# Four weight buffers one word further each, the activations right behind them, and two masks read as one spread column

## The chip, the cores and the metric

The kernel runs on one core of a Trainium2 chip. The time is the device time of one execution in microseconds (us); smaller is better. A core has a matrix engine (TensorE, PE in the rows; its weight loads are PEld), a vector engine (VectorE, DVE), a scalar engine (ScalarE, ACT), a small general engine (GpSimd, POOL) and a queue engine (SyncE, SP). All of them work on one on-chip memory of 128 partitions, in which every tensor has a byte address that is the same in each partition.

## The reference

The reference is a float32 forward pass over 256 tokens of width 1024: two model blocks after each other. The first has an attention layer with compressed, selected and windowed keys (NSA), a convolutional feed-forward layer, a state-space layer (SSD) and a second feed-forward layer. The second has a gated delta rule layer (GDN) with attention to a memory, and a gated feed-forward layer. Cut to what matters here:

```python
def conv_ffn(h, w_up, conv_w, conv_b, w_down):
    u = causal_dwconv(h @ w_up, conv_w, conv_b)
    val, gate = u[..., :FFN_HIDDEN], u[..., FFN_HIDDEN:]     # FFN_HIDDEN = 2816
    return (jax.nn.silu(gate) * val) @ w_down

x = x + rms_norm(mixer(rms_norm(x, g0)), g1)                 # NSA, then SSD, then GDN + memory
x = x + rms_norm(ffn(rms_norm(x, g2)), g3)                   # three times
```

Nearly all arithmetic is in the products of the 256 rows with some 45 million weights, each of which is read once.

## The kernel before

The weights come as 176 chunks of up to 2048 columns by 128 partitions, in the order in which they are used. SyncE loads chunk i into `raw[i % 3]`. ScalarE rounds it into `whi[i % 4]` (L520) and VectorE, for 12 chunks GpSimd, writes the rest, raw minus high, into `wlo[i % 4]` (L528, L536). The activations are held in the same two parts, transposed, in `xT[0]` and `xT[1]` for the input of a layer, in `gT` for the hidden layer of a feed-forward part, in `yT` and `yG` for the outputs of SSD and GDN, and in `mT` for the memory rows. Every product is then three matmuls (L539 to L541, `pe_three`), which add up in the same bank of the accumulators:

```python
def pe_three(e, out, a, b, start, stop):
    e.matmul(out, a[1], b[0], start=start, stop=False)
    e.matmul(out, a[0], b[1], start=False, stop=False)
    return e.matmul(out, a[0], b[0], start=False, stop=stop)
```

The first operand is loaded into the array as weights (stationary, 128 columns), the second is streamed past it (moving). In the rows `bank<-xT,whi` means that `xT` is moving and `whi` is stationary. There are three uses:

- `pe_fm`: a piece of the chunk is stationary (128 columns) and `xT[:, k, :]` is moving (256 columns). The two loops over 22 chunks in each feed-forward part ("up") are of this kind, as are most projections.
- `pe_tm`: `xT[:, k, 128 s:128 s + 128]` is stationary and a chunk piece of 256 columns is moving.
- `pe_down`: a piece of `gT`, `yT`, `yG` or `xT` is stationary and 512 columns of a chunk are moving.

Each matmul has a weight load of its own, and the load of the next runs while the present one streams. The steps in `k` are 1024 bytes apart in the operands with 256 columns, the two halves of a piece 512 bytes. The order of the layers' pieces is written out by hand for each engine in NSA, SSD and GDN; the feed-forward parts are plain loops.

Where the tensors lie follows from the order in which they are declared, each rounded up to 32 bytes. In bytes from the start of a partition, with the remainder of a division by 512 that the prediction uses:

| tensor | before | remainder | after | remainder |
|---|---|---|---|---|
| `whi[i]` | 41088 + 8192 i | 128 | 41088 + 8196 i | 128 + 4 i |
| `wlo[i]` | 73856 + 8192 i | 128 | 74368 + 8196 i | 128 + 4 i |
| `xT[0]`, `xT[1]` | 128960, 137152 | 448 | 108096, 116288 | 64 |
| `masks` | 110144 | 64 | 152576 | 0 |
| `gT` | 157760, 180288 | 64 | the same | 64 |
| `yT`, `yG`, `mT` (all six) | 157760 to 211008 | 64 | the same | 64 |

`half` holds two masks of 128 by 128, ones in the rows of the lower or of the upper 64 partitions. They are stationary operands of L1685, L1686 and L2228 alone.

Of the kernel before, what the change touches and what calls it, by code (L numbers as in the profile page):

```python
# [97 lines left out]
    _ROWS[_n] = (_o, _w)  # L98
    _o += _w
_NROW = _o  # L100
_MASKS = 6 * 128 + 8 * 64 + 8


def _host_masks():

    a = np.arange(128)
    r, c = a[:, None], a[None, :]
    same = (r // 64) == (c // 64)
    m = [r == c, r <= c, (r <= c) & same, same, (r < 64) & (c >= 0), (r >= 64) & (c >= 0)]
    m = [x.astype(np.float32) for x in m]  # L110

    r, c = r % 64, np.arange(64)[None, :]
    for b in (1, 2, 4, 8, 16, 32):
        m.append(((r // (2 * b) == c // (2 * b)) & (r % (2 * b) < b) & (c % (2 * b) >= b)).astype(np.float32))
    m += [(r == c).astype(np.float32), (r <= c).astype(np.float32)]

    m.append((a[:, None] // 15 == np.arange(8)[None, :]).astype(np.float32))
    return np.ascontiguousarray(np.concatenate(m, 1))
# [138 lines left out]
PW, NRAW, NHL, AHEAD = 1024, 3, 4, 3  # L257


def build(nc, wall, x_d, mem_d, cols_d, rows_d, masks_d, neg_d, out_d):  # L260
    f32 = mybir.dt.float32
    f32r = mybir.dt.float32r
# [17 lines left out]
    with root:  # L280
# [20 lines left out]
        def sb(shape, dt=f32, st=root, name="t"):  # L301
            names[0] += 1
            return st.enter_context(nc.sbuf_tensor(f"{name}{names[0]}", shape, dt))
# [2 lines left out]

        banks = [root.enter_context(nc.psum_tensor(f"bank{i}", [128, 512], f32)) for i in range(8)]
        raw = [sb([128, 2048], name="raw") for _ in range(NRAW)]
        whi = [sb([128, 2048], f32r, name="whi") for _ in range(NHL)]
        wlo = [sb([128, 2048], f32r, name="wlo") for _ in range(NHL)]  # L310
        cols = sb([128, _NCOL], name="cols")
        masks = sb([128, _MASKS], name="masks")
        negf_w = 2 * 128 + 64 + 30 + 8 + 4 + 1
        negb = sb([128, negf_w - 1], bf16, name="negb")
        identb = sb([128, 128], bf16, name="identb")
        valid = sb([128, 2], name="valid")
        srow = sb([128, 32 + 32 + 16], name="srow")
        grow = sb([128, 1024], name="grow")
        nhalf = sb([128, 1], name="nhalf")
        h = sb([128, 2, 1024], name="h")  # L320
        xT = [sb([128, 8, 256], f32r, name="xT") for _ in range(2)]
        ss = sb([128, 8], name="ss")
        rr = sb([128, 4], name="rr")
        sqj = sb([128, 1024], name="sqj")
        xs = sb([128, 1024], name="xs")
        grow2 = sb([128, 1024], name="grow2")
        sb([128, 16], name="space")
        gains = (grow, grow2)
        ident, tri, tri64, blk64 = (masks[:, 128 * i:128 * i + 128] for i in range(4))
        half = [masks[:, 512:640], masks[:, 640:768]]  # L330
        level, (idc, tric) = ([masks[:, 768 + 64 * i:832 + 64 * i] for i in v] for v in (range(6), range(6, 8)))
        ones1 = masks[:, 255:256]
        own8 = masks[0:120, 1280:1288]
        neg_qk, neg_sl, neg_gd = negb[:, 0:128], negb[:, 128:256], negb[:, 256:320]
        quad, fourth = negb[0:96, 350:358], negb[0:96, 358:362]

# [112 lines left out]
        for i in range(2):  # L449
            c = {n: sb([128, 4, 128], st=gd, name=n) for n in ("kbg", "kg", "vb")}  # L450
# [2677 lines left out]
```

## Time and profile before

| | |
|---|---|
| three runs | 1198.19, 1198.83, 1201.48 us; median 1198.83 |
| the profiled execution, its own time | 1202.38 us |
| its span, from the first to the last instruction | 1200.6 us |
| TensorE busy | 1174.5 us, 98% of the span |
| VectorE, ScalarE busy | 847.7 us, 652.0 us |
| granted TensorE clock, mean | 0.999 |
| instructions | 23183 |

A busy TensorE is not TensorE at its peak: matmuls overlap, and each is shown with its whole latency (some 280 ns for 256 columns), so its pace is read from the start of one to the start of the next, or by counting how many fall into a stretch.

### The profile page before, as it was taken

To read this page: it belongs to the slowest core of one execution; us is meant where nothing else is said; L and a number is where in the kernel's file an instruction comes from. 1 tells how busy PE (TensorE), PEld (TensorE's weight loads), DVE (VectorE), ACT (ScalarE), POOL (GpSimd) and SP (SyncE) were. 2 spreads that over 40 slices of the span, in tenths; PEclk is the share of its full clock that TensorE was granted. 3 is DMA by queue.
4 is the path that set the end of the run, shared out by engine and by line. 5 is a ranking of instruction groups with operands and counts; after the bars stand their busy time and mean duration, and the time that the engine had idled before them with its cause. 6 is when DMAs were issued, how large, how long until landed. Compare 5 with 4: busy or idle time off the path is not lost.

```text
span 1200.6 us, 23183 instructions
## 1 busy us (share of the span) xinstructions
PE 1174.5 (98%) x9852; PEld 1078.0 (90%) x9852; DVE 847.7 (71%) x1299; ACT 652.0 (54%) x1171; POOL 151.1 (13%) x143
## 2 busy tenths in 40 slices
PE   8999999999999999999999999999999999999998
PEld 8897789999889898878999988999989878999986
DVE  6678777888557988886788865857577776655542
ACT  4657556666446665744666643665434534645431
POOL 1320000000002332100000000103443401000000
PEclk9999999999999999999999999999999999999999
DMA  8832235565634453352755564452231322755540
GB/s 308 269 141 89 100 104 206 189 210 195 231 106 176 155 183 137 115 184 106 281 180 195 188 233 170 170 185 106 104 110 72 111 94 97 281 186 197 181 174 35
DMA packets 31622, 196.67 MB, mean 164 GB/s; under 512 B 4000, under 2 KB 5664, under 8 KB 9376
## 3 DMA queue, kind: packets, MB, share of 16 engines
q1 hardware_dynamic: 27504, 185.17, 43.6%
q10 hardware_dynamic: 4016, 10.03, 2.6%
q8 instruction: 77, 1.26, 0.4%
q14 instruction: 25, 0.20, 0.0%
HBM read 193.09 MB, written 1.05 MB: 162 GB/s over the span
## 4 chain that ended last, share of the span: by engine, by line
PE 88%; DVE 5%; ACT 3%; issue 2%; POOL 1%; DMA 0%; DVEq 0%; POOLq 0%; ACTq 0%
PE bank L539 24%; PE bank L540 24%; PE bank L541 24%; DVE wlo L528 2%; PE bank L1895 1%; PE bank L1133 1%; PE bank L1190 1%; PE bank L1217 1%; ACT whi L520 1%; PE bank L726 1%; PE bank L2539 1%; PE bank L2482 1%; PE bank L3006 1%; POOL rr L668 0%; PE bank L2497 0%
## 5 line engine op out<-in xcount | busy, mean ns | idle before, releaser
L528 DVE TENSOR_TENSOR wlo<-raw,whi 128x1024 fp32r<-128x1024 f32 x322 | 389.1, 1245 | 88.8 <-ACT whi L520 88.1
L539 PE MATMUL bank<-xT,wlo 128*128 128x256 f32 x1488 | 419.0, 282 | 4.3 <-DVE wlo L528 2.1
L541 PE MATMUL bank<-xT,whi 128*128 128x256 f32 x1488 | 413.7, 278 | 0.0
L540 PE MATMUL bank<-xT,whi 128*128 128x256 f32 x1488 | 413.4, 278 | 0.0
L520 ACT ACTIVATE whi<-raw 128x1024 fp32r<-128x1024 f32 (+1 forms) x349 | 349.3, 1048 | 116.4 <-PE bank L541 89.9
L539 PEld LDWEIGHTS bank<-xT,wlo 128*128 128x128 f32 x1488 | 279.1, 188 | 7.9 <-DVE xc L1602 2.8
L540 PEld LDWEIGHTS bank<-xT,whi 128*128 128x128 f32 x1488 | 279.4, 188 | 0.6 <-issue 0.5
L541 PEld LDWEIGHTS bank<-xT,whi 128*128 128x128 f32 x1488 | 279.3, 188 | 0.0
L668 POOL TENSOR_TENSOR rr<-rr,nhalf 128x1 f32<-128x1 f32 x34 | 24.8, 730 | 710.0 <-DVE rr L656 518.9
L539 PE MATMUL bank<-whi,gT 128*128 128x512 f32 x264 | 103.8, 393 | 0.0
L540 PE MATMUL bank<-wlo,gT 128*128 128x512 f32 x264 | 103.7, 393 | 0.0
L541 PE MATMUL bank<-whi,gT 128*128 128x512 f32 x264 | 102.7, 389 | 0.0
L539 PE MATMUL bank<-whi,xT 128*128 128x256 f32 (+1 forms) x320 | 95.6, 299 | 2.6 <-DVE xT L742 2.6
L540 PE MATMUL bank<-wlo,xT 128*128 128x256 f32 (+1 forms) x320 | 92.6, 289 | 0.0
L541 PE MATMUL bank<-whi,xT 128*128 128x256 f32 (+1 forms) x320 | 92.6, 289 | 0.0
L536 POOL TENSOR_TENSOR wlo<-raw,whi 128x1024 fp32r<-128x1024 f32 x24 | 61.4, 2560 | 118.0 <-ACT whi L520 109.3
L539 PEld LDWEIGHTS bank<-whi,xT 128*128 128x128 f32 x320 | 60.2, 188 | 7.5 <-DVE xT L742 2.8
L540 PEld LDWEIGHTS bank<-wlo,xT 128*128 128x128 f32 x320 | 60.2, 188 | 1.8 <-issue 0.5
L541 PEld LDWEIGHTS bank<-whi,xT 128*128 128x128 f32 x320 | 60.2, 188 | 1.5
L541 PEld LDWEIGHTS bank<-whi,gT 128*128 128x128 f32 x264 | 49.6, 188 | 11.2
L539 PEld LDWEIGHTS bank<-whi,gT 128*128 128x128 f32 x264 | 49.6, 188 | 11.1
L540 PEld LDWEIGHTS bank<-wlo,gT 128*128 128x128 f32 x264 | 49.6, 188 | 9.8
(390 smaller groups left out, 1763.7 us busy)
## 6 DMA issues: line engine op xcount, KB each, us to landing
raw<-in_wall SPq DMA_DIRECT2D x173, 1024.0 KB, 4.9
grow<-in_rows ACTq DMA_DIRECT2D x13, 512.0 KB, 5.3
h<-in_x SPq DMA_DIRECT2D x4, 256.0 KB, 5.2
dsk<-in_rows ACTq DMA_DIRECT2D x4, 256.0 KB, 3.1
memx<-in_mem ACTq DMA_DIRECT2D x1, 1024.0 KB, 10.0
out<-h SPq DMA_DIRECT2D x4, 256.0 KB, 2.0
masks<-in_masks SPq DMA_DIRECT2D x1, 580.0 KB, 13.3
D<-Tx ACTq DMA_DIRECT2D x4, 128.0 KB, 6.0
```

The source lines that it names most:

```text
L520: e.activation(high, src, ACTF.Copy).then_inc(*up("act.high", p))
L528: e.tensor_tensor(low, src, high, SUB).then_inc(*up("dve.low", p))
L536: e.tensor_tensor(low, src, high, SUB).then_inc(*up("pool.low", p))
L539: e.matmul(out, a[1], b[0], start=start, stop=False)
L540: e.matmul(out, a[0], b[1], start=False, stop=False)
L541: return e.matmul(out, a[0], b[0], start=False, stop=stop)
L668: return e.tensor_tensor(v, v, nhalf[:, :].to_broadcast([128, n]), ALU.pow)
L726: r = e.transpose(tl(turn_bank(k, t, n), j), tl(xs_of(k, t), c), ident)
L1133: r = e.matmul(tl(wbank(2 * m + p), i * (t + 1) + kb), qT[rows, 4 * (g // 2) + h0 + i, 128 * t:128 * t + 128], tl(kz[br][rows, g // 2, :], ...
L1190: r = e.transpose(tl(wbank(n), kb * k + i), tl(aP[place(n)], i * (W // 128) + kb), ident)
L1217: r = e.matmul(banks[6 + g // 2][64 * p:64 * p + 64, 128 * h0:128 * h0 + 128 * k], vv[br][:, kb, 64 * (g + p):64 * (g + p) + 64], aPT[(2 * ...
L1895: r = e.matmul(banks[4][:, 64 * i:64 * i + 64], E[:, i, :], xdt[:, 64 * i:64 * i + 64], start=True, stop=True)
```

## The change

Only addresses and the two masks change. The four high buffers and the four low buffers become slices of one tensor each, 2049 words apart, so that buffer i begins 4 i bytes further than before. `xT` and the other tensors with the activations are declared directly behind the weights' buffers; `cols`, `masks` and the small bf16 tensors come behind them. The two masks of `half` leave the table of masks (1024 bytes per partition less to load), which makes room for the 1024 bytes that the spacing takes, so the tensors of the single layers stay where they were. `half` is now column 384 and column 511 of the table, each spread over 128 columns with step 0.

```diff
-_MASKS = 6 * 128 + 8 * 64 + 8
+_MASKS = 4 * 128 + 8 * 64 + 8
...
-    m = [r == c, r <= c, (r <= c) & same, same, (r < 64) & (c >= 0), (r >= 64) & (c >= 0)]
+    m = [r == c, r <= c, (r <= c) & same, same]
...
-        whi = [sb([128, 2048], f32r, name="whi") for _ in range(NHL)]
-        wlo = [sb([128, 2048], f32r, name="wlo") for _ in range(NHL)]
+        whi, wlo = ([w[:, 2049 * i:2049 * i + 2048] for i in range(NHL)]
+                    for w in (sb([128, 2080 * NHL], f32r, name=n) for n in ("whi", "wlo")))
+        valid = sb([128, 2], name="valid")
+        srow = sb([128, 32 + 32 + 16], name="srow")
+        nhalf = sb([128, 1], name="nhalf")
+        ss = sb([128, 8], name="ss")
+        rr = sb([128, 4], name="rr")
+        xT = [sb([128, 8, 256], f32r, name="xT") for _ in range(2)]
+        h = sb([128, 2, 1024], name="h")
+        sqj = sb([128, 1024], name="sqj")
+        xs = sb([128, 1024], name="xs")
+        grow = sb([128, 1024], name="grow")
+        grow2 = sb([128, 1024], name="grow2")
         cols = sb([128, _NCOL], name="cols")
         masks = sb([128, _MASKS], name="masks")
...
-        half = [masks[:, 512:640], masks[:, 640:768]]
-        level, (idc, tric) = ([masks[:, 768 + 64 * i:832 + 64 * i] for i in v] for v in (range(6), range(6, 8)))
+        half = [masks[:, c:c + 1].to_broadcast([128, 128]) for c in (384, 511)]
+        level, (idc, tric) = ([masks[:, 512 + 64 * i:576 + 64 * i] for i in v] for v in (range(6), range(6, 8)))
```

## Rows read from the trace of the kernel before

**Rows 1.** The page: busy time by engine, and the granted clock over 40 slices.
```profile
PE 1174.5 (98%) x9852; PEld 1078.0 (90%) x9852; DVE 847.7 (71%) x1299; ACT 652.0 (54%) x1171; POOL 151.1 (13%) x143
PEclk9999999999999999999999999999999999999999
```

**Rows 2.** The page: the chain that ended last, by engine.
```profile
PE 88%; DVE 5%; ACT 3%; issue 2%; POOL 1%; DMA 0%; DVEq 0%; POOLq 0%; ACTq 0%
```

**Rows 3.** Groups of instructions by line and shape: busy us, mean ns of one.
```profile
L541 PE MATMUL bank<-xT,whi 128*128 128x256 f32 x1488 | 413.7, 278 | 0.0
...
L528 DVE TENSOR_TENSOR wlo<-raw,whi 128x1024 fp32r<-128x1024 f32 x322 | 389.1, 1245 | 88.8 <-ACT whi L520 88.1
L520 ACT ACTIVATE whi<-raw 128x1024 fp32r<-128x1024 f32 x346 | 348.2, 1053 | 111.5 <-PE bank L541 89.9 <-DMA raw<-in_wall 15.6 <-issue 5.0
...
L541 PE MATMUL bank<-whi,gT 128*128 128x512 f32 x264 | 102.7, 389 | 0.0
...
L541 PE MATMUL bank<-whi,xT 128*128 128x256 f32 x288 | 80.0, 278 | 0.0
...
L541 PE MATMUL bank<-whi,xT 128*128 128x512 f32 x32 | 12.6, 395 | 0.0
```

**Rows 4.** TensorE in 100 us of each "up" loop: busy us (count), clock, DMA share.
```profile
190.00:290.00 100.00, 100.00 (x885) 1.00 0.57 193
590.00:690.00 100.00, 100.00 (x851) 1.00 0.55 190
1033.00:1133.00 100.00, 100.00 (x884) 1.00 0.58 204
```

**Rows 5.** TensorE in order of time, ahead of and in the first "up" loop.
```profile
186.83 0.28 PE L541 MATMUL bank<-xT,whi 128*128 128x256 f32 x1
...
187.19 0.28 PE L541 MATMUL bank<-xT,whi 128*128 128x256 f32 x1
187.30 0.60 PE L849 MATMUL bank<-masks,xs 128*128 128x128 f32 x4
...
187.98 0.28 PE L541 MATMUL bank<-xT,whi 128*128 128x256 f32 x1
...
188.66 0.28 PE L541 MATMUL bank<-xT,whi 128*128 128x256 f32 x1
```

**Rows 6.** TensorE in order of time, the memory rows' projection, `mT` moving.
```profile
759.85 0.28 PE L541 MATMUL bank<-mT,whi 128*128 128x256 f32 x1
...
760.53 0.28 PE L541 MATMUL bank<-mT,whi 128*128 128x256 f32 x1
```

**Rows 7.** TensorE's 512-column matmuls in two stretches, by `gT` and by `xT`.
```profile
295.00:345.00 50.00, 50.00 (x220) 1.00 0.58 210
153.00:159.00 6.00, 6.00 (x27) 1.00 0.00 0
```

**Rows 8.** TensorE in order of time, inside GDN: `xT` moving.
```profile
839.95 0.28 PE L541 MATMUL bank<-xT,whi 128*128 128x256 f32 x1
...
840.30 0.28 PE L541 MATMUL bank<-xT,whi 128*128 128x256 f32 x1
```

**Rows 9.** Five stretches, busy us (count): PE, PEld, DVE, ACT, POOL; clock, DMA share.
```profile
20.00:49.00 29.00, 29.00 (x250) 29.00 (x250) 19.92 (x25) 14.35 (x17) 10.47 (x11) 1.00 0.90 280
49.00:109.00 60.00, 55.47 (x475) 49.75 (x473) 43.20 (x77) 39.09 (x102) 8.84 (x8) 1.00 0.44 157
354.00:429.00 75.00, 71.06 (x585) 67.41 (x583) 60.78 (x95) 46.59 (x83) 20.43 (x13) 1.00 0.48 173
584.00:691.00 107.00, 107.00 (x911) 107.00 (x910) 89.59 (x140) 70.23 (x101) 0.00 (x0) 1.00 0.55 190
779.00:1010.00 231.00, 228.18 (x2842) 208.86 (x2839) 154.05 (x293) 112.52 (x235) 68.41 (x62) 1.00 0.32 114
```

**Rows 10.** TensorE in order of time: operands that begin off a 16-byte line.
```profile
76.01 1.05 PE L1329 MATMUL bank<-cols,grow 128*120 128x64 f32 x8
76.90 0.28 PE L1190 MATMUL bank<-masks,P 128*128 128x128 f32 x1
```

**Rows 11.** VectorE by line and shape: operands shifted by one or two words.
```profile
L911 DVE SCALAR_TENSOR_TENSOR cv<-bank,cols,cv 128x255 f32<-128x255 f32 x44 | 19.1, 475 | 2.6 <-ACT cv L899 2.6
L911 DVE SCALAR_TENSOR_TENSOR cv<-bank,cols,cv 128x254 f32<-128x254 f32 x44 | 19.0, 473 | 0.0
```

**Rows 12.** Most of the matmuls of `half` (min/median/max ns), and the load of the masks.
```profile
L2228 PE MATMUL bank<-gg,masks x8: 256/256/256, 791.4 to 792.6; 128*128 128x8 f32 x8
masks<-in_masks SPq DMA_DIRECT2D x1, 580.0 KB, 13.3
```

**Rows 13.** TensorE in order of time: transposes, one load and 128 columns each.
```profile
10.48 1.04 PE L726 MATMUL bank<-masks,xs 128*128 128x128 f32 x8
```

More of the change, by code:

```diff
@@ L315, in build @@
         identb = sb([128, 128], bf16, name="identb")
[L316 to L326, printed above, removed]
         sb([128, 16], name="space")
@@ L329, in build @@
         ident, tri, tri64, blk64 = (masks[:, 128 * i:128 * i + 128] for i in range(4))
-        half = [masks[:, 512:640], masks[:, 640:768]]
-        level, (idc, tric) = ([masks[:, 768 + 64 * i:832 + 64 * i] for i in v] for v in (range(6), range(6, 8)))
+        half = [masks[:, c:c + 1].to_broadcast([128, 128]) for c in (384, 511)]
+        level, (idc, tric) = ([masks[:, 512 + 64 * i:576 + 64 * i] for i in v] for v in (range(6), range(6, 8)))
         ones1 = masks[:, 255:256]
-        own8 = masks[0:120, 1280:1288]
+        own8 = masks[0:120, 1024:1032]
         neg_qk, neg_sl, neg_gd = negb[:, 0:128], negb[:, 128:256], negb[:, 256:320]
```

## The prediction, on record before the change was run

> **What bounds the kernel now.** I read the page first. TensorE is busy 98% of the span, at full clock (2.4 GHz) throughout [rows 1], and the chain that ended last runs through it for 88% [rows 2]. The three matmul lines of `pe_three` carry that, 1488 of each with 256 columns of a 128-partition activation moving and the rest of other forms [rows 3]. So a change of addresses can matter only where it changes the pace of these matmuls, or delays an engine that feeds them.
>
> The mean duration of one matmul (278 ns) says nothing of the pace, since they overlap. I therefore counted them, in the three "up" loops, which run the same code over the same buffers. In 100 us each there are 885, 851 and 884 [rows 4]. Some two of each count lie across an edge, so the paces are 100/883 = 113.3 ns, 100/849 = 117.8 ns and 113.3 ns. TensorE never idles in any of them. VectorE and ScalarE are busy in like measure in the first two, and DMA share is 0.57 against 0.55, so neither explains the 4.4 ns. The order of time shows where the pace changes: between 186.83 and 187.19 us three matmuls take 0.36 us (120 ns, with rounding), then come four transposes, and between 187.98 and 188.66 us six take 0.68 us (113 ns) [rows 5]. Nothing but a short break in the stream lies between. The second loop has the same break and stays at the slow pace. There are two steady paces, then, and a break draws between them.
>
> The operands' place seems to set the odds. With `mT` moving, six matmuls take 0.68 us, again 113 ns [rows 6]. With 512 columns moving and `gT` stationary, 220 fall in 50 us, so 50/218.5 = 228.8 ns; with `xT` stationary 27 in 6 us, at most 6/25.5 = 235 ns, about 233 when the edges are shared out [rows 7]. That is again some 4.4 ns more. In GDN, three with `xT` moving take 0.35 us, 117 ns [rows 8]. What sets `xT` apart is its address. Divided by 512 the weights' buffers leave 128 and the tensors of the single layers (`gT`, `mT`, `yT`, `yG`) leave 64, but `xT` leaves 448. I take 512 as the largest period that can matter, because steps of 1024 bytes in `k` and of 512 between halves change no pace inside a run. Two loops with `xT` at the fast pace show that the place does not decide it alone.
>
> **The change, part by part.**
>
> *xT moves.* Its remainder becomes 64, that of `mT` and `gT`. If the odds go with it, each slow matmul gives back 4.4 ns. The second "up" loop has 911 in its stretch [rows 9]: 911 x 4.44 = 4.0 us. Outside the three loops there are 1488 - 3 x 304 = 576 groups of three with `xT` moving [rows 3, 9]. The samples in the mixed stretches are almost all slow, so I take nine in ten: 0.9 x 576 x 3 x 4.44 = 6.9 us. The form with `xT` stationary is mixed in the timeline; I take a quarter of its 288 groups, 1.0 us, and the 32 groups of 512 columns give 0.4 us [rows 3]. That is 12.3 us in all. Not all arrives. Up to 49 us DMA is busy 0.90 of the time [rows 9] and the chunks set the pace: 0.8 us is lost there. In the written-out stretches TensorE is busy 92 to 99% [rows 9] and some of its work is waited for by ScalarE and VectorE and back, so I pass on three quarters: 0.75 x (12.3 - 4.0 - 0.8) = 5.6 us. Sum: 4.0 + 5.6 = 9.6 us.
>
> *The buffers begin 4, 8 or 12 bytes further.* No three-part matmul of before reads an operand off a 16-byte line, so this is bounded from both sides. Nearest is L1329, whose moving operand begins 4 bytes past such a line: eight start within 76.90 - 76.01 = 0.89 us, 111 ns each, no more than a transpose on aligned operands, which is 110 ns (eight in 1.04 us, four in 0.60, so four in 0.44) [rows 5, 10, 13]. From that row I take nothing. The upper bound for a plain cost is one column more per operand, 1 / 1.2 GHz = 0.8 ns, in three of four buffers: 0.75 x 3 x (1488 + 288 + 264 + 32) x 0.8 = 3.7 us [rows 3]. A gain can't be excluded either: if the shift takes the two streams out of each other's way altogether, a 256-column matmul could pace like a transpose, 110 ns (the fourth case below). The engines that write there: VectorE's shifted operands cost 475 ns for 255 elements and 473 for 254, which begin one and two words off [rows 11], so nothing; and it is busy only 84% of the "up" loops' time [rows 9].
>
> The Trainium skill speaks against the whole first part. "SBUF — State Buffer", section "Who interferes with whom", says that TensorE has two read ports of its own, one for the moving operand and one for weight loads, and that it never waits on anyone. By it addresses are without effect, the two paces have another origin, and the sum is 0. The trace doesn't settle it: two paces over the same addresses speak for the page, `xT` against `gT` and `mT` speaks against it.
>
> *Two masks become a column.* They are 12 small matmuls, of which the eight of L2228 stand in the rows [rows 12]. A spread column costs what the mask did, within 10 ns each: 0.1 us at most. The load shrinks by 128 KB of 580 and lands 13.3 us after issue [rows 12], some 19 us into the span; TensorE does not idle from 20 to 49 us [rows 9], so nothing waits for it and the gain is nothing. If that cover were gone it would be 128/580 of the 13.3 us, 2.9 us.
>
> *Moved tensors that only others use* (`h`, `xs`, `cols`, `masks`): transposes already pace by their weight load, 110 ns [rows 13]. Nothing.
>
> **Against the runs.** The sum is made against the profiled execution: 1202.4 - 9.6 = 1192.8 us. The three runs lie 3.3 us apart at most, and the profiled one 3.6 above their median, about what one loop at the other pace is worth (4.0). So the median run has perhaps that loop fast already, and I would expect 1193 for the changed kernel, 5.8 below the median.
>
> **The rivals.**
>
> *Addresses decide nothing* (the page's rule as a mechanism: breaks alone draw the pace). For it: the two paces of the same loop [rows 4], and runs apart by about one loop. Against it: `mT` and `gT` [rows 6, 7]. New addresses leave the odds, and the time is 1198.8, give or take one loop at half chance, 1196.5 to 1201.
>
> *The shift spoils three buffers of four.* A stream that passes from chunk to chunk now changes its distance to `xT` by 4 bytes and falls out of the fast pace. For it: the fast state is a locked one, lost at a small break [rows 5]. Then the first and third loop, now fast, turn slow in three quarters: 0.75 x 2 x 911 x 4.44 = 6.1 us; the move of `xT` gives nothing, and half of the 3 x 264 matmuls with `gT` [rows 3] lose as much each, 1.8 us. That is 1202.4 + 7.9 = 1210.3 us. It decides from the point at which over half of the shifted chunks run slower than 115.5 ns.
>
> *A word costs a column.* The first mechanism holds, with the 3.7 us of the upper bound: 1192.8 + 3.7 = 1196.5.
>
> *The streams stop disturbing each other.* All 256-column matmuls go from some 115.5 ns, halfway between the paces, to 110: 3 x (1488 + 288) x 5.5 = 29 us, and those with `gT` from 228.8 to twice 110 ns: 792 x 8.8 = 7 us [rows 3, 7]. Three quarters of it: 1202.4 - 27 = 1175. For it speaks only that transposes do it [rows 13]. "TensorE: Matmul & The Clock Gate" of the Trainium skill, section "Wait — 56ns, not 53.3ns?", gives N / 2.4 + 2.5 ns per matmul at full clock, 109.2 ns at 256 columns; the trace has 113.3 at its best.
>
> **How the numbers follow.** Chances: first mechanism at its size 0.40, with a column's cost 0.12, addresses decide nothing 0.20, spoiled buffers 0.20, undisturbed streams 0.08. 0.3% is 3.6 us, about what a measurement of this kernel can tell from no change: the bounds are 1195.2 and 1202.4. Faster are nine tenths of the first case (0.36), a quarter of the column's (0.03), the fourth case (0.08) and lucky draws of the second (0.05): 0.52. Slower are the spoiled buffers but for 0.01, and unlucky draws, 0.04: 0.23. The rest, 0.25, is the same. The predicted time is the first case's, 1193, its own range 1189 to 1197. The range goes from 1183, more than halfway to the undisturbed streams, to 1207, most of the way to the spoiled buffers; it leaves out 0.06 below and 0.13 above.
>
> **What the profile after would show.** If I am right: some 882 to 885 matmuls in every 100 us of all three "up" loops, about 229 ns for the 512-column ones with `xT`, 113 ns with `xT` moving in GDN, and unchanged durations of L520 and L528 (1053 and 1245 ns) [rows 3]. A count of 851 in the second loop says that the place of `xT` is not it; chunks in turn of different pace (one in four fast) say that the shift spoils it; a pace between 113.3 and 115 in all says that a word costs a column; a count of over 900 the fourth case. The prediction is wrong if breaks rather than places draw the pace, or if the written-out stretches give the saved time back as waits.

## The result

The changed kernel takes 1211.91 us, median of four runs from 1211.41 to 1212.39; the kernel before took 1198.51 us beside it (1197.87 to 1201.48). The ratio is 1.0103, with a 95% interval from 1.0085 to 1.012. It is slower by 13.4 us, where 1193 us and a range up to 1207 us had been forecast. The profiled execution took 1212.39 us, with a span of 1210.6 us, 10.0 more than the profiled one of before (which was one of the slower runs of before).

The page after, its span, busy times and chain by engine, against [rows 1, 2]:

```profile
span 1210.6 us, 23183 instructions
PE 1184.1 (98%) x9852; PEld 1084.6 (90%) x9852; DVE 844.9 (70%) x1299; ACT 651.7 (54%) x1171; POOL 145.0 (12%) x143
PE 88%; DVE 5%; ACT 3%; issue 2%; POOL 1%; DMA 1%; DVEq 0%; ACTq 0%; POOLq 0%
```

The same number of instructions, the same shares of the chain within a percent, and 9.6 us more of busy TensorE. VectorE and ScalarE are busy no longer than before. So the time did not come in as a wait: the matmuls themselves pace differently. The groups by line and shape, against [rows 3]:

```profile
L541 PE MATMUL bank<-xT,whi 128*128 128x256 f32 x1488 | 415.0, 279 | 0.0
...
L528 DVE TENSOR_TENSOR wlo<-raw,whi 128x1024 fp32r<-128x1024 f32 x322 | 388.3, 1242 | 94.1 <-ACT whi L520 93.5
L520 ACT ACTIVATE whi<-raw 128x1024 fp32r<-128x1024 f32 x346 | 348.5, 1054 | 115.4 <-PE bank L541 97.4 <-DMA raw<-in_wall 12.9 <-issue 4.1
...
L541 PE MATMUL bank<-whi,gT 128*128 128x512 f32 x264 | 104.3, 395 | 0.0
```

The writers L520 and L528 do not notice the shift (1054 and 1242 ns, as forecast). The mean duration of the 512-column matmul with `gT` grew from 389 to 395 ns, that of the 256-column one by 1 ns. Since matmuls overlap, durations are only a hint, and the pace is counted. TensorE in the three "up" loops (tile `xT`), with the columns of [rows 4], and then the 512-column matmuls with `gT` in the same 50 us as in [rows 7]:

```profile
190.00:290.00 100.00, 100.00 (x863) 1.00 0.56 193
590.00:690.00 100.00, 100.00 (x865) 1.00 0.55 193
1043.00:1143.00 100.00, 100.00 (x864) 1.00 0.58 201
295.00:345.00 50.00, 50.00 (x217) 1.00 0.57 196
```

All three loops now have the same count, 864, which stands between the 885 and the 851 of before. With `gT` it is 217 for 220. An even count can hide a mixture. The same view inside four chunks that follow each other in the first loop, 5 us in each, buffers 0, 1, 2 and 3:

```profile
200.40:205.40 5.00, 5.00 (x47) 1.00 0.74 277
206.00:211.00 5.00, 5.00 (x45) 1.00 0.39 120
211.60:216.60 5.00, 5.00 (x44) 1.00 0.71 254
217.20:222.20 5.00, 5.00 (x47) 1.00 0.49 149
```

Two chunks of four are slow, and they are the ones that begin 4 and 8 bytes further; the one with 12 bytes is as fast as the one with none. The DMA share is not the cause: 0.74 and 0.49 belong to the fast ones, 0.39 and 0.71 to the slow ones. In order of time, two L539 of the chunk in buffer 0 and then two of the chunk in buffer 1:

```profile
200.28 0.28 PE L539 MATMUL bank<-xT,wlo 128*128 128x256 f32 x1
...
205.05 0.28 PE L539 MATMUL bank<-xT,wlo 128*128 128x256 f32 x1
...
206.09 0.28 PE L539 MATMUL bank<-xT,wlo 128*128 128x256 f32 x1
...
210.71 0.28 PE L539 MATMUL bank<-xT,wlo 128*128 128x256 f32 x1
```

The second is the 42nd matmul after the first, 4.77 us later, 113.6 ns each; the fourth is the 39th after the third, 4.62 us later, 118.5 ns each.

Sorted by buffer over the whole trace, from the start of one matmul to that of the next, in ns. The forms are those of the kernel's section: fm has `xT` moving (4464 matmuls), tm has `xT` stationary and 256 columns of the weights moving (864), and "512" is `gT` stationary and 512 columns moving (792; with `yT`, `yG` and `xT` 1224). Rows e1 to e6 are the experiments below. The first few matmuls after a break start further apart, so a mean lies a little above the steady pace (113.7 for 113.3 in e4).

| kernel | fm, buffers 0 to 3 | tm, buffers 0 to 3 | 512 with `gT`, 0 to 3 |
|---|---|---|---|
| before | 115.5 116.3 115.6 115.6 | 114.1 115.8 115.6 114.8 | 228.9 229.0 228.9 229.0 |
| after | 114.0 118.4 118.3 114.5 | 116.3 117.9 121.2 117.7 | 229.0 236.6 235.4 228.6 |
| e1, move, no shift | 115.3 115.4 114.7 115.1 | 117.4 117.8 117.8 116.3 | 228.9 to 229.0 |
| e2, shift, no move | 117.7 118.2 119.0 119.8 | 116.4 121.9 120.3 118.4 | 229.1 236.7 235.4 228.6 |
| e4, moved, all 12 further | 113.7 113.9 113.7 113.6 | 117.6 to 117.8 | 228.3 to 228.5 |
| e5, moved, all 4 further | 118.3 in all | 119.1 to 120.4 | 237.7 to 238.0 |
| e6, not moved, all 12 further | 121.2 120.0 120.0 121.1 | 118.4 to 118.7 | 228.3 to 228.4 |

Before, the mean of fm is a mixture of 113.3 and 117.8, by stretch and not by buffer. The difference of before and after, from the means of the four buffers: fm 116.3 - 115.75 = 0.55 ns x 4464 = 2.5 us; 512 columns 232.4 - 229.0 = 3.4 ns x 1224 = 4.2 us; tm 118.3 - 115.1 = 3.2 ns x 864 = 2.8 us. That is 9.5 us, and the spans differ by 10.0.

The masks, against [rows 12], do what was forecast: the load is 452 KB and lands 13.2 us after issue, the eight matmuls still take 256 ns each, and TensorE does not idle from 20 to 49 us.

```profile
L2228 PE MATMUL bank<-gg,masks x8: 256/256/256, 796.5 to 797.7; 128*128 128x8 f32 x8
masks<-in_masks SPq DMA_DIRECT2D x1, 452.0 KB, 13.2
20.00:49.00 29.00, 29.00 (x248) 29.00 (x247) 19.46 (x25) 14.34 (x17) 9.39 (x11) 1.00 0.94 291
```

### The profile page after: what moved, and what is told of

Same layout as the page of the kernel before. It is cut to its first block, busy times and chain, and to the rows that moved or that the text cites. A ratio compares the mean times of both kernels' runs of the same rounds, so it can differ in the third digit from the quotient of the medians.

```text
span 1210.6 us, 23183 instructions
## 1 busy us (share of the span) xinstructions
PE 1184.1 (98%) x9852; PEld 1084.6 (90%) x9852; DVE 844.9 (70%) x1299; ACT 651.7 (54%) x1171; POOL 145.0 (12%) x143
## 4 chain that ended last, share of the span: by engine, by line
PE 88%; DVE 5%; ACT 3%; issue 2%; POOL 1%; DMA 1%; DVEq 0%; ACTq 0%; POOLq 0%
PE bank L539 24%; PE bank L541 24%; PE bank L540 24%; DVE wlo L528 2%; PE bank L1895 1%; PE bank L1133 1%; PE bank L1190 1%; PE bank L1217 1%; ACT whi L520 1%; PE bank L726 1%; PE bank L2539 1%; DMA grow<-in_rows 1%; PE bank L2482 1%; PE bank L2497 0%; PE bank L2526 0%
## 5 line engine op out<-in xcount | busy, mean ns | idle before, releaser
L528 DVE TENSOR_TENSOR wlo<-raw,whi 128x1024 fp32r<-128x1024 f32 x322 | 388.3, 1242 | 94.1 <-ACT whi L520 93.5
L539 PE MATMUL bank<-xT,wlo 128*128 128x256 f32 x1488 | 420.6, 283 | 4.3 <-DVE wlo L528 2.3
L520 ACT ACTIVATE whi<-raw 128x1024 fp32r<-128x1024 f32 (+1 forms) x349 | 349.6, 1048 | 120.3 <-PE bank L541 97.4
L539 PEld LDWEIGHTS bank<-xT,wlo 128*128 128x128 f32 x1488 | 280.1, 188 | 8.0 <-DVE xc L1602 2.7
L539 PE MATMUL bank<-whi,gT 128*128 128x512 f32 x264 | 104.2, 395 | 0.0
L539 PE MATMUL bank<-whi,xT 128*128 128x256 f32 (+1 forms) x320 | 96.2, 301 | 2.5 <-DVE xT L742 2.5
L536 POOL TENSOR_TENSOR wlo<-raw,whi 128x1024 fp32r<-128x1024 f32 x24 | 56.5, 2356 | 120.2 <-ACT whi L520 111.5
L539 PEld LDWEIGHTS bank<-whi,xT 128*128 128x128 f32 x320 | 60.4, 189 | 7.3 <-DVE xT L742 2.7
L539 PEld LDWEIGHTS bank<-whi,gT 128*128 128x128 f32 x264 | 49.6, 188 | 11.5
```

What stands on the lines that cost most here:

```text
L520: e.activation(high, src, ACTF.Copy).then_inc(*up("act.high", p))
L528: e.tensor_tensor(low, src, high, SUB).then_inc(*up("dve.low", p))
L536: e.tensor_tensor(low, src, high, SUB).then_inc(*up("pool.low", p))
```

## The experiments

**One part at a time.** The change has three parts, and three kernels hold one each (e2 and e3 share the spread column). e1 is the changed kernel with the buffers at their old starts within 32 bytes:

```diff
-        whi, wlo = ([w[:, 2049 * i:2049 * i + 2048] for i in range(NHL)]
+        whi, wlo = ([w[:, 2048 * i + o:2048 * i + o + 2048] for i, o in enumerate((0, 0, 0, 0))]
```

> The changed kernel with all four buffers at 0 bytes further (they stay slices of one tensor per part, xT at the same place as in the changed kernel). Theory A (the move of xT helps, the shift by 4 and 8 bytes hurts): every buffer runs at the fast pace, some 113.5 ns per 256-column matmul with xT moving and 229 ns per 512-column one, and the time is 1189 to 1195 us, 4 to 9 below before. Rival B (the move of xT or of the other tensors is what costs): 1205 us or more with all four buffers alike. Rival C (places decide nothing, only draws): within 4 us of before, with one or more up loops at 117.8 ns.

e2 is the kernel before, with its order of tensors, and only the spaced buffers and the spread column:

```diff
-        whi = [sb([128, 2048], f32r, name="whi") for _ in range(NHL)]
-        wlo = [sb([128, 2048], f32r, name="wlo") for _ in range(NHL)]
+        whi, wlo = ([w[:, 2049 * i:2049 * i + 2048] for i in range(NHL)]
+                    for w in (sb([128, 2080 * NHL], f32r, name=n) for n in ("whi", "wlo")))
```

> The kernel before with the shifted buffers and the spread column, but with xT, h, cols and the others in their old order, so xT at its old place (remainder 448). Theory A: buffers at +4 and +8 bytes are slow (118 ns and 235 to 237 ns) and those at 0 and +12 are as before or slower for want of the move, 1212 to 1220 us. Rival B (the move costs, the shift is free): 1195 to 1202 us, all buffers alike.

e3 is the kernel before with the spread column, and a pad that keeps all that follows at its address:

```diff
         masks = sb([128, _MASKS], name="masks")
+        sb([128, 256], name="pad")
...
-        half = [masks[:, 512:640], masks[:, 640:768]]
+        half = [masks[:, c:c + 1].to_broadcast([128, 128]) for c in (384, 511)]
```

> The kernel before with the two masks read as a spread column, and a pad in place of their 1024 bytes, so that every other tensor stays where it was. All theories: 1197 to 1202 us, no difference that can be measured. If the masks mattered, 3 us or more to either side, at L1685, L2228 or in the first 20 us.

e4 is the changed kernel with every buffer 12 bytes further. It asks whether it matters that the buffers differ, or only where each of them stands:

```diff
-        whi, wlo = ([w[:, 2049 * i:2049 * i + 2048] for i in range(NHL)]
+        whi, wlo = ([w[:, 2048 * i + o:2048 * i + o + 2048] for i, o in enumerate((3, 3, 3, 3))]
```

> The changed kernel with all four buffers 12 bytes further. Theory A in its narrow form (only starts 4 and 8 bytes past a 16-byte line are slow, 12 is as good as 0): all at 114 to 114.5 ns and 228 to 229 ns, 1190 to 1197 us. Rival D (any start off a 16-byte line costs, the fast fourth buffer owes its pace to the one before or behind it): 116 ns or more everywhere, 1208 us or more.

Measured, with the ratio to the kernel before, run beside them (median 1198.63 us), and its 95% interval:

| kernel | median us | from, to | ratio |
|---|---|---|---|
| e1, move only | 1201.42 | 1198.37, 1203.14 | 1.0005 [0.999, 1.0019] |
| e2, shift only | 1221.39 | 1220.78, 1222.24 | 1.0175 [1.0152, 1.0197] |
| e3, masks only | 1198.23 | 1197.47, 1206.35 | 0.9994 [0.9978, 1.0011] |
| e4, all 12 further | 1195.92 | 1195.56, 1197.93 | 0.9965 [0.995, 0.9981] |

The masks are without effect. The move alone is too: it cannot be told from no change. The shift alone costs 1.75% at the old place of `xT`; at the new place it costs 1211.9 - 1201.4 = 10.5 us (9.3 us between the profiled spans, 1210.6 - 1201.3). And e4 is faster than both kernels, with shifted buffers. The same stretch of the first "up" loop, tile `xT`, in e1, in e2 and in e4:

```profile
190.00:290.00 100.00, 100.00 (x885) 1.00 0.56 192
```
```profile
190.00:290.00 100.00, 100.00 (x842) 1.00 0.56 192
```
```profile
190.00:290.00 100.00, 99.77 (x881) 1.00 0.56 190
```

The move did not fix the pace in the loops, as the second one of e1 shows (the first row below: 766 in 90 us, 117.8 ns). In e3, where `xT` stands at its old place, the same loop has 796, 113.4 ns (second row), and in e4 too (third row):

```profile
590.00:680.00 90.00, 90.00 (x766) 1.00 0.53 188
```
```profile
590.00:680.00 90.00, 90.00 (x796) 1.00 0.53 188
```
```profile
590.00:680.00 90.00, 90.00 (x796) 1.00 0.56 193
```

So one loop can go either way at both places of `xT`. The single runs of the kernel before say the same without a trace: of 25 that stood beside e1, 16 lie between 1197.7 and 1199.2 us and nine between 1201.9 and 1203.3, 4 us apart, the price of one loop. Of the seven beside e5 and e6 below, three lie between 1202.6 and 1203.6 and two at 1207.5 and 1207.8, another step of 4 us; no trace was kept of those two, so that they are two slow loops is an inference. The move paid in one form and cost in another: the 32 groups of 512 columns with `xT` went from 233.3 to some 229 ns, as forecast, but tm went from 115.1 to 117.3 ns. The sums for the move: fm (115.75 - 115.1) x 4464 = 2.9 us gained and `xT` with 512 columns 0.4 us; tm 2.2 x 864 = 1.9 us lost. What is left is a gain of 1.4 us; the profiled spans differ by 0.7 us the other way (1201.3 and 1200.6), and the spread of single runs is 4.

**The pace measured by itself.** Do the weights' bytes matter alone, the activations' alone, or the distance between them? m1 leaves the whole reference out. It runs 96 matmuls in the order of `pe_three` for each pair of places, with four transposes between two runs, while no other engine works (from 40 to 800 us ScalarE, VectorE and GpSimd are busy 0.00 us, and the DMA share is 0.00):

```python
def run(e, out, st, mv, n):
    for j in range(n // 3):
        k = j % 8
        first, last = j == 0, j == n // 3 - 1
        yield (out, st[1](k), mv[0](k), first, False)
        yield (out, st[0](k), mv[1](k), False, False)
        yield (out, st[0](k), mv[0](k), False, last)
```

> A kernel of its own that copies x to the output and times matmuls alone: runs of 96 in the order of pe_three, 256 columns moving and 128 loaded, tensors at the places of the changed kernel. The weights' pair begins 0, 4, 8 or 12 bytes further, the activations' pair too, in all 16 combinations and in both roles (weights stationary; weights moving), each combination twice, with four transposes between. It leaves the whole reference out. Theory L (a start off a 16-byte line costs by itself, 12 bytes being an exception): the pace depends on the weights' shift alone in row and column alike, shift 0 and 12 at 113 to 114 ns, shift 4 and 8 at 117.5 to 120 ns whatever the other operand's. Theory R (only the distance between the two operands counts): pairs with the same difference have the same pace, so both at +4 or both at +8 run at 113 to 114 ns. Theory S (draws at a break alone): the two passes over the same combination differ as much as different combinations.

One line of the trace is one run; the columns are the duration (min/median/max ns), and the start of the first and of the last of 32. Weights stationary, 0, 4, 8 and 12 bytes further, activations at the new place of `xT`:

```profile
L72 PE MATMUL bank<-xh,wh x32: 276/276/278, 37.6 to 48.1; 128*128 128x256 f32 x32
...
L74 PE MATMUL bank<-xh,wh x32: 280/281/281, 49.4 to 60.4; 128*128 128x256 f32 x32
...
L76 PE MATMUL bank<-xh,wh x32: 279/283/285, 61.6 to 72.7; 128*128 128x256 f32 x32
...
L78 PE MATMUL bank<-xh,wh x32: 276/276/281, 73.9 to 84.4; 128*128 128x256 f32 x32
```

31 groups of three lie between the first and the last start: 10.5 us is 113 ns for each matmul, 11.0 us 118 and 11.1 us 119. From the starts in ns the steady paces are 113.3, 118.3, 118.3 and 113.3, the order of the changed kernel's four buffers with nothing else running. The other pairs, x being the activations' bytes further:

| x | fm, weights 0, 4, 8, 12 further | tm, weights 0, 4, 8, 12 further |
|---|---|---|
| 0 | 113.3 118.3 118.3 113.3 | 113.3/117.8 117.8 121.7 117.5 |
| 4 | 121.7 120.0 123.3 121.1 | 118 120.0 120.0 117 to 120 |
| 8 | 120.0 120.0 120.5 120.6 | 116.7 121.2 120.0 118 to 120 |
| 12 | 117.8 118.1 120.0 117.5 | 113.3/120 122.2 119.8 116.7 |

An equal distance does not restore the fast pace: (4, 4) has 120.0 and (8, 8) 120.5. Nor is it the weights' byte alone, since with the activations 4 further all four are slow. It is the pair. And some pairs have two paces; where both passes differ the table gives both. The same pair in tm, in the first and in a later pass of the same kernel:

```profile
L104 PE MATMUL bank<-wh,xh x32: 276/276/278, 234.6 to 245.2; 128*128 128x256 f32 x32
...
L166 PE MATMUL bank<-wh,xh x32: 279/279/281, 616.2 to 627.1; 128*128 128x256 f32 x32
```

**512 columns, and places further off.** m2, which leaves the reference out in the same way, runs the form of `pe_down` and moves the activations by up to 112 words. Against m1, in words:

```diff
-for each x in 0, 1, 2, 3 and w in 0, 1, 2, 3 (words): fm, tm, 256 columns
+for each x in 0, 1, 2, 3 and w in 0, 1, 2, 3: weights moving, 512 columns
+for each x in 4, 8, 12, 16, 20, 24, 28, 32, 48, 64, 80, 96, 112, w = 0: fm, tm
```

> The same kind of kernel: first the 16 combinations with 512 columns of the weights moving, then the activations' pair 0, 16, 32, 48, 64, 80, 96, 112, 128, 192, 256, 320, 384 and 448 bytes further with the weights at 0, in both roles, twice. At 384 the remainders are those of the kernel before (128 and 448), at 0 those of the changed one (128 and 64). Theory P (the remainder by 512 sets the pace): one group of distances at 113.3 ns and another, 384 bytes among them, at 117.8 ns, the same in both passes. Theory S (draws): the two passes disagree about as often as they agree. In the 512-column form shift 4 and 8 of the weights at 235 to 237 ns, 0 and 12 at 228 to 229 ns.

The 512-column form, weights 0, 4, 8 and 12 bytes further, activations at 0:

```profile
L72 PE MATMUL bank<-wh,xh x32: 393/394/397, 37.3 to 58.6; 128*128 128x512 f32 x32
...
L74 PE MATMUL bank<-wh,xh x32: 398/399/402, 60.2 to 82.3; 128*128 128x512 f32 x32
...
L76 PE MATMUL bank<-wh,xh x32: 393/397/400, 83.9 to 105.8; 128*128 128x512 f32 x32
...
L78 PE MATMUL bank<-wh,xh x32: 389/389/391, 107.3 to 128.6; 128*128 128x512 f32 x32
```

The steady paces are 228.9, 236.7, 235.5 and 228.3 ns, within 0.3 of what the changed kernel has with `gT` in its four buffers. The places further off, weights at 0: fm has 113.3 with the activations at 0 and at 64 words (256 bytes), and 116.7 to 120.0 at all of the twelve others up to 112 words; 80, 96 and 112 words (120.0, 117.8, 118.7) repeat 16, 32 and 48 (120.0, 117.8, 118.6). So for fm the period is 256 bytes, within the 512 that the prediction took as the largest. tm has 113.3 at 32 words and 117.8 at 0 and at 64 in both passes (one run of m1 had 113.3 at 0): the new place of `xT` is good for fm and mostly bad for tm. tm does not repeat as cleanly, since its pairs have several paces as well: at 96 words 117.8 and then 113.3, at 28 words 117.7 and then 123.2.

m3, again with the reference left out, moves the weights too, and takes the old place of `xT`, which stands 96 words from the new one:

```diff
+for each w in 0, 3, 16, 32, 35, 48, 64, 67, 96, 99 (words), x = 0: fm, tm, 512 columns
+for each w in 0, 1, 2, 3, x = 96: fm, tm, 512 columns
```

> The same kind of kernel, with the activations' pair at its place in the changed kernel and the weights' pair 0, 12, 64, 128, 140, 192, 256, 268, 384 and 396 bytes further, in the three forms, each twice; between them the activations' pair at the place of the kernel before (384 bytes further) with the weights 0, 4, 8 and 12 bytes further. Theory R (the distance between the operands, modulo 256 bytes, sets the pace): weights 128 bytes further behave like activations 128 bytes nearer, so 117.8 ns with the activations moving and 113.3 ns with the weights moving, and 256 bytes further is as 0. Theory Q (each operand's own place counts): the weights at 64 and 192 bytes are not what the activations at those were (120.0 and 118.7 ns). For the kernel with the shift alone: at least three of its four buffers at 118 ns or more with the activations moving.

With x = 0, fm has 113.3 with the weights at 0, 12, 128 and 256 bytes (and at 268), 118.8 and 120.0 at 64 and 192, 120.0 at 140 and 396. That repeats after 256 bytes and not after 128 or 64. The first pair (weights 0, `xT`'s new place) ran at 113.3 at first and at 117.8 in the second pass, so it too has two paces:

```profile
L72 PE MATMUL bank<-xh,wh x32: 276/276/277, 37.0 to 47.6; 128*128 128x256 f32 x32
...
L214 PE MATMUL bank<-xh,wh x32: 281/281/281, 1161.4 to 1172.3; 128*128 128x256 f32 x32
...
L138 PE MATMUL bank<-xh,wh x32: 276/276/276, 546.5 to 557.0; 128*128 128x256 f32 x32
```

The last row is the old place with the weights 12 bytes further: 113.3 ns in its one run. With the weights 0, 4 and 8 bytes further the old place has 117.8, 117.7 and 116.7. That is already not what e2 shows in its four buffers (117.7 118.2 119.0 119.8), and the expectation of 118 or more in three of four failed: one run of each pair tells the 4-byte buffers within 0.5 ns, and the 12-byte one is off by 6.5. For tm the same four are 113.3 121.7 120.1 118.6, against 116.4 121.9 120.3 118.4 in e2.

**Two tests of the table.** If the pair decides, a kernel whose four buffers all stand 4 bytes further should be slow without any difference between buffers. If what costs is the passage from one buffer to another that lies differently, as a rival of the prediction had it, it should be as fast as e4:

```diff
-        whi, wlo = ([w[:, 2049 * i:2049 * i + 2048] for i in range(NHL)]
+        whi, wlo = ([w[:, 2048 * i + o:2048 * i + o + 2048] for i, o in enumerate((1, 1, 1, 1))]
```

> The changed kernel with all four buffers 4 bytes further. By the table of the matmuls measured alone (118.3 ns with the activations moving, 117.8 to 118.7 ns with the weights moving, 236.6 ns with 512 columns) against the kernel with all at 12 bytes (113.7, 117.6, 228.4 ns, 1195.9 us): 4464 x 4.6 + 864 x 0.6 + 1224 x 8.2 ns = 31 us more at the most, 1218 to 1228 us. Rival (it is the mix of places from chunk to chunk that costs, and a uniform shift is free): 1195 to 1203 us.

It took 1227.09 us (1226.25 to 1228.14), against 1203.44 for the kernel before beside it (1198.55 to 1207.75), ratio 1.0192 [1.0159, 1.0226]. The first "up" loop, tile `xT`:

```profile
190.00:290.00 100.00, 100.00 (x847) 1.00 0.57 192
```

118.3 ns in every buffer, and 238 for 512 columns (a mixture of 236.5 and 240.0, by chunk): the shift costs by itself, with no passage between unlike buffers. Against e1: (118.3 - 115.1) x 4464 = 14.3 us, (237.8 - 229.0) x 1224 = 10.8 us, (119.7 - 117.3) x 864 = 2.1 us, 27 us in all, of which the span shows 1224.4 - 1201.3 = 23.1.

The last kernel asks the table for a good pair at the old place of `xT`, the kernel before with all buffers 12 bytes further, and the spread column:

```diff
-        whi = [sb([128, 2048], f32r, name="whi") for _ in range(NHL)]
-        wlo = [sb([128, 2048], f32r, name="wlo") for _ in range(NHL)]
+        whi, wlo = ([w[:, 2048 * i + o:2048 * i + o + 2048] for i, o in enumerate((3, 3, 3, 3))]
+                    for w in (sb([128, 2080 * NHL], f32r, name=n) for n in ("whi", "wlo")))
```

> The kernel before with the spread column and all four buffers 12 bytes further, xT at its old place. By the table (113.3 ns with xT moving, 118.7 ns with the weights moving, 231 ns with 512 columns and xT, 228.3 ns with gT): 1195 to 1198 us, like the one with all at 12 bytes at the new place. Rival (the buffer at 12 bytes is slow at the old place, as the fourth buffer of the kernel with the shift alone was, 119.8 ns): 1210 us or more. If the table holds here, that buffer was slow by what it inherited from the chunks ahead of it.

The table failed here. It took 1226.54 us (1224.61 to 1228.22), ratio 1.0191 [1.0149, 1.0232], and the first "up" loop, tile `xT`, has the lowest count of all kernels here:

```profile
190.00:290.00 100.00, 100.00 (x813) 1.00 0.55 187
```

By the starts that is 123.3 ns throughout the first loop; in the second and in the third it is 120.1, whatever the buffer, though the chunk just ahead of each ran at 123.4, and 120.6 is the mean over the kernel. The 512-column form with `gT` stayed at 228.4. The sum holds: fm (120.6 - 115.75) x 4464 = 21.7 us, tm (118.5 - 115.1) x 864 = 2.9 us, 512 columns 0.6 x 1128 = 0.7 us gained: 23.9, against 1223.2 - 1200.6 = 22.6 us of span. So the paces explain this time as well; what fails is to foretell the pace of this pair from one run of 96 matmuls.

**One pair, several paces.** The trace of e6 shows why. The same form with the same pair of places also runs at the fast pace, in a chunk ahead of the first loop; 4 us of it, then 4 us in the first loop and 4 us in the second:

```profile
40.00:44.00 4.00, 4.00 (x37) 1.00 0.99 383
213.00:217.00 4.00, 4.00 (x34) 1.00 0.75 256
613.50:617.50 4.00, 4.00 (x36) 1.00 0.30 82
```

By the starts these are 113.3, 123.3 and 120.1 ns. The fast chunk is the one with the DMA share of 0.99, so a busy DMA is not what makes this pair slow. Sorted in this way, the steady pace of fm in every unbroken stretch of one chunk (24 or 48 matmuls) of all kernels:

| weights further, place of `xT` | kernels | paces in ns (number of stretches) |
|---|---|---|
| 0, old | before, e3 | 113.3 (104), 117.8 (124) |
| 0, old | e2, buffer 0 | 117.8 (27) |
| 0, new | e1; after, buffer 0 | 113.3 (90), 117.8 (50) |
| 4, new | e5; after, buffer 1 | 118.3 (147) |
| 4, old | e2, buffer 1 | 117.3 to 117.8 (13), 118.1 to 118.5 (20) |
| 8, new | after, buffer 2 | 118.0 to 118.6 (27) |
| 8, old | e2, buffer 2 | 116.7 (5), 117.5 to 117.8 (5), 120.0 (16) |
| 12, new | e4; after, buffer 3 | 113.3 (128), 120.0 (12) |
| 12, old | e6; e2, buffer 3 | 113.3 (11), 119.7 to 120.3 (94), 123.1 to 123.5 (36) |

Three stretches with a pause in them are left out. So the pair decides which paces can occur, and something in the sequence of the work picks one. The neighbours may have a part in that: at the old place the unshifted pair ran fast in 104 of 228 stretches where all four buffers lay alike, and in none of 27 between shifted buffers (e2). But a whole loop mostly keeps one pace, so these are far fewer draws than stretches.

## Why the prediction was wrong

The frame held: TensorE bounds the kernel, only the pace of `pe_three` matters, and the time follows from paces and counts (9.5 us summed, 10.0 measured). That the pace of one pair goes between 113.3 and 117.8 at a short break was read rightly too. Two terms of the sum failed.

*The buffers 4, 8 and 12 bytes further* is the step that decided the sign. The prediction took nothing and at most 3.7 us; the runs show 10.5 us at the new place (after against e1; 9.3 by their spans) and some 20 us at the old place (spans of e2 and before, 1220.4 - 1200.6). The value came from L1329, eight matmuls of 64 columns with plain float32 operands [rows 10], of which only the moving one lies off a line. They start 111 ns apart, as transposes with twice their columns do [rows 5, 13], so by these rows the number of columns does not bound them, and they could not show what an unaligned operand costs where streaming is the bound. The upper bound, one column more, had no row behind its form, and its 0.8 ns is not what a column costs in these rows: (228.8 - 113.3) / 256 = 0.45 ns [rows 4, 7]. Measured at the new place are 5 ns for 256 columns and 6.5 to 9 for 512 at 4 and 8 bytes, and next to nothing at 12 bytes. A cost that is not even monotone in the shift is not a column per word.

*The move of `xT`*, 12.3 us and 9.6 passed on, measured nothing (1.0005). Its premise, that the odds of the fast pace go with the remainder in every form, rested on three small samples (`mT`, `gT`, one piece of GDN) [rows 6 to 8] of forms whose partners differ. The odds did move, but not in one direction. Outside the three loops fm ran fast in 4 of 57 stretches before, as the prediction's nine in ten had it, and in 30 of 57 in e1, not in all. The 32 groups of 512 columns with `xT` did go to 229 ns, 0.4 us. With `xT` stationary the new place is slow (22 of 26 stretches at 117.8 in e1, 7 of 26 before; 117.3 for 115.1 in the mean), which the prediction had booked as a gain of 1.0 us. And the second loop, 4.0 of the 9.6 us, still ran at 117.8 in e1. `mT` shows that the remainder does not fix the pace: stationary, it ran at 113.3 before and at 117.8 in e1, with the same remainders of all its operands in both.

The 0.8 us taken off for a start where the chunks set the pace has no row behind it: from 20 us on, TensorE is busy 29.00 of the 29.00 us of that stretch [rows 9].

*The masks and the other moved tensors*: right, nothing (e3, 0.9994).

*The rivals.* "The shift spoils three buffers of four" gave 1210.3 us, close to 1211.9, and its sign in the profile, chunks in turn of different pace, is what is seen. That the number is close is partly luck: it has 6.1 us in fm, 1.8 in 512 columns and none in tm, where 2.5, 4.2 and 2.8 were measured. Its mechanism is at most a part of the loss. e5 has no passage between unlike buffers and is slower, and in the changed kernel two buffers of four are spoiled rather than three. But a passage can cost: the buffer with 12 bytes ran at 120.0 in 5 of its 27 stretches of the changed kernel, and e2's buffer 0 never ran fast. "Addresses decide nothing" has half a truth, since the pace of one pair is drawn at a break in some cases, 4 us per loop. As a rule it fell: e5 and e4 differ by 8 bytes and by 31 us. "A word costs a column" and "the streams stop disturbing each other" found no support; the best paces anywhere are 113.3, and 226.7 for 512 columns (m3, weights at 192 bytes).

The Trainium skill, "SBUF — State Buffer", section "Who interferes with whom", says that TensorE's two read ports are its own and that it never waits on anyone. No run here shows a wait on another engine: m1 has none at work, and the order of its four buffers is that of the changed kernel. But with both ports in use the pace depends on the two addresses, so what the prediction drew from that page, that addresses are without effect, is refuted here. "TensorE: Matmul & The Clock Gate" of the Trainium skill, section "Wait — 56ns, not 53.3ns?", gives N / 2.4 + 2.5 ns, 109.2 for 256 columns; no pair measured here reaches it, the fastest is 113.3.

*Open* is the mechanism: why the pairs settle at 113.3, 116.7, 117.8, 118.3, 120.0, 121.7 or 123.3 ns, and what picks one of a pair's paces. Every matmul here streams one operand while the next one's weights load. That the two reads meet in the memory is a reading that would fit a period of 256 bytes in both, but it is not shown: no run separated it from others (a run with one weight load for many matmuls was not tried).

## What to carry to other kernels

Where TensorE is full, put the byte addresses of both operands on the list of things that are tuned, and measure each pair in the kernel itself: shift all buffers of a pool alike, one variant at a time, and read the starts by buffer and by form. Count how often a pair runs at which pace, since one run of it can show the rarest of three. The best here (e4: moved `xT`, all weights 12 bytes further) has 1195.92 us, 0.9965 [0.995, 0.9981] of the kernel before, while all weights 4 bytes further (e5) have 1.0192 of it. And a neighbour row bounds a cost only if the same thing bounds both: a matmul that paces by something other than its columns says nothing of one that paces by its stream.

## What was not expected of the hardware

- The pace of an fp32r matmul with a weight load beside it depends on the pair of operand addresses: the steady paces go from 113.3 to 123.4 ns for 256 columns and from 226.7 to 240.0 for 512 (240.0 in e5), at a granted clock of 1.00. For fm, where it was measured alone, it repeats after 256 bytes in either operand (four pairs of places each, m2 and m3).
- With the activations at their new place, weights 4 and 8 bytes further cost 5 ns per 256 columns and 6.5 to 9 per 512. 12 bytes further cost nothing there in 128 of 140 stretches, and 7 to 10 ns more than 113.3 in 130 of 141 at the old place.
- The same pair can hold either of two or three steady paces (113.3 and 117.8; 113.3, 120 and 123.3) for a whole loop of 100 us, and change at a break as short as four transposes. In the kernel before that spreads single runs over 4 us, 0.3%, by the one loop whose pace was seen to change, and the seven runs beside e5 and e6 lie 9 us apart.
